# Column tiles of 32 instead of 64 in the SSD products of decay and inputs

## What is computed

```python
seg = a_cs[:, :, :, None] - a_cs[:, :, None, :]
decay = jnp.exp(jnp.where(causal, seg, -jnp.inf))
cb = jnp.einsum('bclgn,bcsgn->bclsg', Cc, Bc)
y_diag = jnp.einsum('bclsg,bclsgr,bcsgrp->bclgrp', cb, decay, x)
```

## Time and profile before

| what | us |
|---|---|
| median of three runs | 1371.86 |
| the profiled execution's own time | 1373.83 |
| its span, first to last instruction | 1372.0 |
| TensorE busy in it | 1286.4 |
| granted TensorE clock, mean | 0.981 of full |

### The profile page before, as it was taken

How to read it: one execution, slowest core, us unless ns; L and a number is a source line. 1 busy time by engine, 2 the same in 40 slices (tenths; PEclk the granted TensorE clock), 3 DMA queues, 4 the chain that set the end, 5 groups by cost and what they waited for, 6 DMA issues and landing times.

```text
span 1372.0 us, 19280 instructions
## 1 busy us (share of the span) xinstructions
PE 1286.4 (94%) x7645; PEld 933.9 (68%) x7645; DVE 587.5 (43%) x960; ACT 374.8 (27%) x746; POOL 703.9 (51%) x719
## 2 busy tenths in 40 slices
PE   5999989899999999999999999999994899999992
PEld 5888867787788777888888877788782334333330
DVE  1144262438893573626764788413325111110113
ACT  4111263412333583112224433601121111111110
POOL 6477644567575402767772656775930333333320
PEclk9999999999999999999999999999996999999996
DMA  6523210342233200242222123722282899999955
GB/s 219 157 77 104 87 57 7 114 161 71 92 113 103 93 2 1 97 165 79 89 77 77 63 71 146 302 73 86 92 368 77 326 372 380 373 380 375 370 219 193
DMA packets 85453, 216.39 MB, mean 158 GB/s; under 512 B 23716, under 2 KB 32628, under 8 KB 71796
## 3 DMA queue, kind: packets, MB, share of 16 engines
q1 hardware_dynamic: 62124, 199.22, 39.3%
q0 software_dynamic: 13824, 8.44, 2.1%
q10 hardware_dynamic: 9416, 7.51, 1.7%
HBM read 255.99 MB, written 26.22 MB: 206 GB/s over the span
## 4 chain that ended last, share of the span: by engine, by line
PE 79%; DVE 5%; DMA 4%; POOL 4%; ACT 3%; issue 3%; DVEq 1%; POOLq 1%; SPq 0%; ACTq 0%
PE ps L141 17%; PE ps L143 17%; PE ps L142 17%; PE ps L1090 10%; PE ps L1102 5%; DMA w_gu<-w_up,over_u 2%; POOL w_lo L1137 2%; PE ps L782 2%; PE ps L1082 1%; POOL w_hi L1134 1%; PE ps L900 1%; PE ps L646 1%; PE ps L908 1%; PE ps L984 1%; DMA back<-y_scratch 1%
## 5 line engine op out<-in xcount | busy, mean ns | idle before, releaser
L1137 POOL TENSOR_TENSOR w_lo<-stage,w_hi 128x512 fp32r<-128x512 f32 (+1 forms) x296 | 398.7, 1379 | 11.1 <-issue 0.7
L1134 POOL CAST w_hi<-stage 128x512 fp32r<-128x512 f32 (+1 forms) x296 | 194.5, 700 | 392.3 <-PE ps L143 372.7
L141 PE MATMUL ps<-hi,w_hi 128*128 128x512 f32 (+1 forms) x600 | 233.9, 390 | 1.3 <-DVEq L1629 0.7
L143 PE MATMUL ps<-lo,w_hi 128*128 128x512 f32 (+1 forms) x600 | 231.9, 387 | 0.0
L142 PE MATMUL ps<-hi,w_lo 128*128 128x512 f32 (+1 forms) x600 | 231.8, 386 | 0.0
L141 PE MATMUL ps<-w_hi,hi 128*128 128x512 f32 (+2 forms) x520 | 184.8, 355 | 4.9 <-POOL w_lo L1137 4.3
L143 PE MATMUL ps<-w_lo,hi 128*128 128x512 f32 (+2 forms) x520 | 183.5, 353 | 0.0
L142 PE MATMUL ps<-w_hi,lo 128*128 128x512 f32 (+2 forms) x520 | 183.5, 353 | 0.0
L1090 PE MATMUL ps<-w_gu,xT 128*64 128x512 f32 x768 | 172.0, 600 | 4.6 <-DMA w_gu<-w_up,over_u 3.3
L141 PEld LDWEIGHTS ps<-hi,w_hi 128*128 128x128 f32 x600 | 112.7, 188 | 28.1 <-issue 3.1
L2245 DVE TENSOR_TENSOR xT<-ps,ffn_kp 128x1024 f32<-128x1024 f32 x24 | 29.4, 1224 | 238.1 <-PE ps L1090 147.8
(11 more groups left out here) (440 smaller groups left out, 1692.8 us busy)
## 6 DMA issues: line engine op xcount, KB each, us to landing
stage<-w_in SPq DMA_DIRECT2D x84, 512.0 KB, 4.4
w_gu<-w_gate SPq DMA_DIRECT2D x32, 1024.0 KB, 11.5
w_gu<-w_up SPq DMA_DIRECT2D x32, 1024.0 KB, 13.7
w_dn<-w_down SPq DMA_DIRECT2D x32, 1024.0 KB, 9.6
stage<-w_out SPq DMA_DIRECT2D x16, 512.0 KB, 4.2
stage<-w_ssd_branch SPq DMA_DIRECT2D x16, 512.0 KB, 4.8
stage<-w_in SPq DMA_DIRECT2D x20, 256.0 KB, 3.0
stage<-w_attn_branch SPq DMA_DIRECT2D x8, 512.0 KB, 4.2
```

The costliest lines, as they stand in the source:

```text
L141: pe.matmul(out, x[0], w[0], start=first, stop=False)
L143: return pe.matmul(out, x[0], w[1], start=False, stop=last)
L1134: nc.gpsimd.tensor_copy(hi[:, b, k, 0:n], stage[:, b, k, 0:n])
L1137: last = nc.gpsimd.tensor_tensor(lo[:, b, k, 0:n], stage[:, b, k, 0:n], hi[:, b, k, 0:n].bitcast(F32), ALU.subtract)
```

## The change

One line: the 128 output tokens of a head are taken in four parts of 32 instead of two of 64. The number of calls goes from 64 to 128 for a chunk, each with half the stationary columns; moving operand, destination, order of heads and the one semaphore increment stay.

```diff
                 for h in range(32):
-                    for l in (slice(0, HD), slice(HD, P)):
+                    for l in (slice(32 * i, 32 * (i + 1)) for i in range(4)):
                         last = pe.matmul(ps[s][l, h // 8, HD * (h % 8):HD * (h % 8 + 1)], decay[:, h, l], xd[:, h, :],
                                          start=True, stop=True)
                 last.then_inc(turn_full, 1)
```

## The result

The changed kernel takes 1376.09 us, median of 20 runs (1371.96 to 1379.91), against 1372.79 for the kernel before, median of 20 (1370.62 to 1377.44). The ratio is 1.0022, with a 95% interval from 1.0013 to 1.0032: slower by 3.0 us, between 1.8 and 4.4. The forecast was 0.4 us less, the range ended at 1374.0.

What follows compares the result with a forecast made beforehand. TensorE was taken to bound the kernel, busy 1286.4 of 1372.0 us. Savings of 0.12 + 0.026 - 0.013 = 0.13 us a chunk, over three chunks 0.4, gave 1371.86 - 0.4 = 1371.5 us; range 1370.2 to 1374.0.

Steps and rivals of the forecast that it cites:

- what sets the pace: L984: step set by loading stationary columns, 58.3 ns; after the change by moving columns, 56.5 ns; 0.13 us saved a chunk.
- a tile of 32 columns has the same moving work as a tile of 64: L984: either tile passes 64 moving columns a head, so only the load in its shadow becomes shorter.
- rival (b): L984: packing counts in full, four tiles doing in one step what two did in two; 1366.3 us; chance 0.03.
- (c): L984: no gain, the matmul step is 58.3 ns for 64 moving columns too; 1371.9 us; chance 0.10.
- three of four groups are on the path: L984 groups of chunks 0, 1 and 2 are on the chain of waits, 11.6 us together.
- the last is covered: Chunk 3: TensorE waits for GpSimd anyway, 1.36 and 2.10 us, so cost or gain up to some 3 us vanishes.
- the cost of fetching: TensorE's instructions: 1024 more records, 66 KB, four packets of 16 KB; nothing added to the sum.
- speed of delivery: L984: 8 records a step, one per 7.1 ns, 512 in succession, can be delivered at no cost.
- the two bounds on delivery: L984, 512 records: above, 14.4 ns each, 7.37 us a group; below, 4 ns from L942's start, 2.1 us, no cost.
- a packet's transfer time: Instruction queue q8: one 16 KB packet takes about 1.1 us, by its share of the DMA engines.
- Rival (a): L984, chunks 0 to 2: delivery bounds the group, 26 ns between matmul starts; +8.8 us, 1380.7 us; chance 0.17.
- Rival (d): L984: partial delivery, 7.1 to 9.1 ns a record; 0 to +2.7 us, at its middle 1373; chance 0.05.

Runs made afterwards that it cites:

- run of spare calls: Kernel before, plus two runs of 384 spare matmul calls (1536 instructions each), behind the second attention and in the expert stage: 1418.67 us, run once.
- doubled groups: Changed kernel with each group's 128 calls made twice (1024 instructions a group): 1407.25 us, median of two runs, ratio 1.0244.

## Why the prediction was wrong

**Right: what sets the pace.** The step was to go from the load's 58.3 ns to the moving operand's 56.5. In the group without a pause it's 56.2 by the matmuls and 55.4 by the loads, so 0.17 us a group was gained where 0.13 was forecast. That a tile of 32 columns has the same moving work as a tile of 64, so that nothing is halved, held as well; rival (b) is out, and so is (c), a step that stays at 58.3. That three of four groups are on the path and that the last is covered held too.

**Wrong: the cost of fetching, and with it the speed of delivery.** This is the step that failed. The forecast's sum adds nothing for the fetching of instructions. That term was my estimate, and no run of the changed kernel shows it: measured are stops of 1.5, 0.3 and 1.4 us in the three groups on the path. In the trace of before each packet of q8 lands at least 7.4 us ahead of the first instruction of the next block; at the three stops of the changed kernel it is 1.3 to 1.5 us. And of the two bounds on delivery I took the lower, from L942's burst of 12 records, because it was the nearest row in shape. It was near in shape and far in length. What it showed is how close together twelve records can start, 4 ns each; what counts for 512 is how fast new ones come in, and where pauses follow each other in the traces that is a block of 256 each 3.5 to 5.1 us, 13.5 to 20 ns an instruction. The forecast of 7.1 ns an instruction held for the 402 instructions up to the pause of chunk 0, and not for the 512.

The number was within reach. The profile of before has q8 with 60 packets of 16 KB and TensorE with 15290 records, from which the prediction has 64 bytes each: 256 instructions a packet, 3.73 us at the pace of L984. The question that I didn't ask is how long a packet is on its way. No row of before shows TensorE waiting for one. The prediction has a packet's transfer time, 1.1 us, and that was right (0.97 to 1.20 us in the table of packets). It isn't the whole of the way: with what comes before and behind it, from the begin of one block to the begin of the next, the table has 3.1 us and more.

**Rival (a)** had the sign and the place, but not the mechanism. A floor under each matmul would have cost 2.9 us in every group, evenly. Measured are +1.34, +0.14 and +1.19 in the three groups on the path, the added time all at borders. Its +8.8 us is three times too much. Rival (d), partial delivery, came to +2.7 at most and is nearest in size. That is luck: it supposed 7.1 to 9.1 ns for every record, and measured are 7 ns a record and stops between blocks.

**The sum, corrected.** Per group: -0.17 for the step, from first to last start (3.56 against 3.73), +1.5, +0.3 and +1.4 for the pauses in chunks 0, 1 and 2. That is 2.7 us, and the timed runs have 3.0 (1.8 to 4.4).

| kernel | added on the path by its trace, us | ratio of timed runs |
|---|---|---|
| the change | 2.7 | 1.0022 (1.0013 to 1.0032) |
| the change, shifted by 136 | 2.2 | 1.0029 (1.0017 to 1.0041) |
| before, shifted by 136 | 0 | 1.0000 (0.9988 to 1.0012) |
| four tiles in chunks 0 and 2 | 2.5 | 1.0025 (1.0013 to 1.0036) |
| four tiles in chunks 1 and 3 | 0.4 | 1.0006 (0.9993 to 1.0019) |
| four tiles in 0 and 2, shifted by 128 | 1.2 | 1.0009 (0.9999 to 1.0019) |

The middle column is the lengthening against before of the groups in chunks 1 and 2, from first to last start, and in chunk 0 of the time from the group's first start to the next `spread` (L962), which takes in the stops at L954 and L1001. The second row's interval begins at 2.3 us, just above its 2.2; the others hold their value.

No version was found that beats the kernel before. An estimate: with every pause out of the way the change would be worth 3 x 0.17 = 0.5 us, far less than the 6.8 us between the fastest and the slowest of 20 runs of one kernel, and it would depend on the count of all instructions ahead.

## What to carry to other kernels

Before an operation is cut into more and smaller instructions, divide the time of the dense run by its instructions, and compare with what the traces show of the supply. Here TensorE got a block of 256 instructions in 3.46 to 3.76 us in the run of spare calls at a DMA share of 0.02 or 0.03, which is 13.5 to 14.7 ns an instruction, and in 4.0 to 5.1 us in the doubled groups at a share of 0.33 to 0.78; the two blocks ahead of the changed kernel's pauses took 3.3 and 3.1 us. At 14.6 ns an instruction the kernel before had no pause in its groups; at 7 ns the changed kernel had stops in three of its four. The burst of twelve records at 4 ns each in L942 did not show it. What showed it were waits named "issue", 1.3 and 1.1 us long, in the middle of a run without semaphores, 7 x 256 instructions apart. 34 harmless calls (136 instructions) ahead of the loop told it apart from other causes: the pauses left chunks 0 and 2, and one of 1.47 us came up in chunk 1.

## What the hardware showed that was not expected

- Only the next block came ahead of its use. In none of the eleven traces does a packet of q8 start more than 43 instructions ahead of the block before the one that it is taken to bring. In the doubled group of chunk 0 a block's work lasted 1.99 us, and the next began 5.10 and 4.00 us after it had begun, with one packet of q8 in each such stretch (766.73 and 770.57 us); with several blocks in flight the second would have come closer to the first.
- TensorE started 512 records in 3.56 us in chunk 3, 7 ns each, about twice as fast as the 13.5 to 14.7 ns an instruction at which blocks came with the DMA engines nearly idle.
- The 26.0 ns between matmul starts that rival (a) read from L942 is no floor across tiles: 256 starts in 3.56 us are 14 ns apart on average. No run here tests it for a single tile.
- In two pause-ridden runs the granted clock fell. In the run with spare calls it was 0.60 of full from 563.35 to 567.08 us, and the same 128 matmuls were busy for 3.01 instead of 1.99 us. It came behind a pause of 3.1 us. The block still took 3.73 us, since the slower work filled the time in which TensorE would have stood. In the doubled groups it was 0.62 and 0.64 in the two last rows shown above, each behind a pause of 2.0 us; after a pause of 3.1 us in chunk 0 it was still at full, and fell 1 us behind the next one, of 2.0 us.
- In the spare run of the expert stage five short stops of 0.5 to 0.7 us stand near its first border. They are not explained.
